# Four-quarter inverse products in the RWKV-7 stage, spaced reloads on the SP queue, and halved weight splits in the sliding-window stage

## The reference, cut to what matters

```
def step(state, inp):
    r_t, w_t, k_t, v_t, kk_t, a_t = inp
    sa = jnp.einsum("bhvk,bhk->bhv", state, -kk_t)
    state = (state * w_t[:, :, None, :]
             + sa[..., None] * (kk_t * a_t)[:, :, None, :]
             + v_t[..., None] * k_t[:, :, None, :])
    y = jnp.einsum("bhvk,bhk->bhv", state, r_t)
    return state, y
```

## Time and profile before

| | us |
|---|---|
| median of 3 runs | 1948.91 |
| lowest and highest | 1947.67, 1950.61 |
| the profiled execution: its own time | 1947.52 |
| its span | 1945.6 |
| around the span | 1.9 |
| PE busy | 1919.5 (99%) |
| DVE busy | 1332.9 (69%) |
| ACT busy | 838.4 (43%) |
| RWKV-7 products, first to last | 204.91 to 383.42 |

### The profile page before, as it was taken

The page is one execution under the profiler, slowest core; times in us unless marked ns, Lnnn a source line. Parts: engine busy times, 40 slices in busy tenths (PEclk is TensorE's granted clock), DMA queues, the critical chain, the costliest instruction groups (busy, mean ns, idle before and its releaser), DMA issues.

```text
span 1945.6 us, 32866 instructions
## 1 busy us (share of the span) xinstructions
PE 1919.5 (99%) x14082; PEld 1653.4 (85%) x14082; DVE 1332.9 (69%) x1751; ACT 838.4 (43%) x1257; POOL 118.7 (6%) x126
## 2 busy tenths in 40 slices
PE   8999999999999999999999999999999999999998
PEld 6877897888788998978989888898887778898897
DVE  5576868576687777676545687677566768777665
ACT  4243744254453444443324454344345545344342
POOL 1155100000000000020000000000002300000000
PEclk9999999999999999999999999999999999999999
DMA  8222404137132332333220223233242113233231
GB/s 270 88 65 66 136 10 143 36 120 130 44 109 87 109 104 92 104 94 108 89 86 26 84 89 107 87 108 109 87 139 73 49 44 109 87 108 109 87 108 44
DMA packets 138641, 182.12 MB, mean 94 GB/s; under 512 B 4853, under 2 KB 103365, under 8 KB 138112
## 3 DMA queue, kind: packets, MB, share of 16 engines
q1 hardware_dynamic: 135392, 168.91, 26.8%
q0 software_dynamic: 3104, 11.11, 2.8%
HBM read 172.66 MB, written 7.34 MB: 93 GB/s over the span
## 4 chain that ended last, share of the span: by engine, by line
PE 94%; DVE 3%; ACT 1%; issue 1%; DMA 0%; DVEq 0%; ACTq 0%
PE X L1579 20%; PE M L1491 19%; PE M L1492 19%; PE M L1493 19%; PE X L642 3%; PE M L1552 1%; PE M L1554 1%; PE M L1553 1%; PE M L1905 1%; PE X L1882 1%; PE X L1762 1%; PE X L1893 1%; PE X L1731 1%; DVE w_lo L2372 1%; PE X L1493 0%
## 5 line engine op out<-in xcount | busy, mean ns | idle before, releaser
L1492 PE MATMUL M<-u,raw_lo 128*128 128x512 f32 x728 | 287.9, 396 | 0.0
L1491 PE MATMUL M<-u,w_hi 128*128 128x512 f32 x728 | 287.9, 395 | 0.0
L1493 PE MATMUL M<-u,w_hi 128*128 128x512 f32 x728 | 286.1, 393 | 0.0
L1995 ACT ACTIVATE w_hi<-raw 128x2048 fp32r<-128x2048 f32 x113 | 215.6, 1908 | 96.2 <-PE M L1554 43.5
L2050 ACT ACTIVATE us<-X 128x256 f32<-128x256 f32 x156 | 60.2, 386 | 426.9 <-PE X L1579 426.9
L2522 DVE TENSOR_TENSOR h<-h,M 128x512 f32<-128x512 f32 x184 | 123.7, 685 | 144.6 <-PE M L1493 144.5
L1579 PE MATMUL X<-t,w_hi 128*128 128x256 f32 x936 | 173.2, 282 | 0.0
L1493 PEld LDWEIGHTS M<-u,w_hi 128*128 128x128 f32 x728 | 137.6, 189 | 32.8
L1491 PEld LDWEIGHTS M<-u,w_hi 128*128 128x128 f32 x728 | 136.8, 188 | 30.8
L1492 PEld LDWEIGHTS M<-u,raw_lo 128*128 128x128 f32 x728 | 136.7, 188 | 29.8
L2372 DVE TENSOR_TENSOR w_lo<-raw,w_hi 128x2048 fp32r<-128x2048 f32 x56 | 128.1, 2289 | 32.5 <-ACT w_hi L1995 32.5
(11 more groups left out here) (529 smaller groups left out, 4564.5 us busy)
## 6 DMA issues: line engine op xcount, KB each, us to landing
raw<-in_w_up_dram SPq DMA_DIRECT2D x48, 1024.0 KB, 5.4
raw<-in_w_down_dram SPq DMA_DIRECT2D x48, 1024.0 KB, 5.1
raw<-in_w_in_dram SPq DMA_DIRECT2D x12, 1024.0 KB, 8.3
raw<-in_a_w_in_dram SPq DMA_DIRECT2D x12, 1024.0 KB, 5.3
h<-in_x_dram SPq DMA_DIRECT2D x16, 256.0 KB, 7.7
raw<-in_w_mk_dram SPq DMA_DIRECT2D x4, 1024.0 KB, 5.1
raw<-in_w_mv_dram SPq DMA_DIRECT2D x4, 1024.0 KB, 5.4
raw<-in_w_out_dram SPq DMA_DIRECT2D x4, 1024.0 KB, 6.5
```

Of the source, the lines that this page charges most:

```text
L1491: mm(dst, wh, xh, start=start, stop=False)
L1492: mm(dst, wl, xh, start=False, stop=False)
L1493: return mm(dst, wh, xl, start=False, stop=stop)
L1995: nc.scalar.activation(hi_of(n)[:, :, :], raw[:, n % 4], ACT.Copy).then_inc(S["w_hi_ready"], 1)
```

## The change

Three edits go together.

**Products on four quarters.** `P2`, `PT2`, `P4`, `PT4` and `TT2` join `RW_QUAD`. The first two read blocks on the chunk's rows and write to the head's rows (`to_heads`); the others read on the head's rows and write back to the chunk's (`to_chunks`). Since `TT2` now needs its right operand on head rows, a new product `PTH` (`P` times the identity, four quarters) makes it for each pair, and DVE adds the identity when it takes it out of PSUM. The three order tables are new. PSUM readers take two banks as one operand (`rw_wide`), same elements as before.

```diff
-RW_QUAD = ("L", "RBT", "AKT", "RKT", "MT", "RT", "N", "Y")
+RW_QUAD = ("L", "RBT", "AKT", "RKT", "MT", "RT", "N", "Y", "P2", "PT2", "PTH", "P4", "PT4", "TT2")
-    tA.0.0 fill.22 bonus.1.2 fill.23 tBd.1.1 RBT.0.2 PT2.0.3 P2.0.1 RBT.1.2 P2.1.3 PT2.1.0 PT4.0.1 TT2.0.2 P4.0.0 PT4.1.3
+    fill.14 fill.15 kk2.1.1 fill.16 fill.17 fill.18 bonus.0.0 tKd.0.1 L.0.1 AKT.0.2 tA.0.0 kk2.2.1 tBd.0.0 fill.19 X.0.2 P2.0.2
...
+            to_heads = dict(P2=("PT", "P"), PT2=("P", "PT"), PTH=("P", "I"))
+            to_chunks = dict(P4=("PT2", "P2"), PT4=("P2", "PT2"), TT2=("P2", "PTH"))
...
+                elif st in to_heads or st in to_chunks:
+                    for cp in range(4):
+                        for turn in range(2):
+                            for cpar in range(2):
+                                hh, at_ = cpar ^ turn, (hp, cpar ^ turn, cp, cpar)
+                                if st in to_chunks:
+                                    a_, b_ = (by_row(n, *at_) for n in to_chunks[st])
+                                    last = mm(quad(st, hp, hh, cpar, cp), a_, b_, start=True, stop=True)
+                                else:
+                                    a_, b_ = (by_chunk(n, *at_) for n in to_heads[st])
+                                    last = mm(quad(st, hp, cpar, hh, cp), a_, b_, start=True, stop=True)
...
+                elif op == "PTH":
+                    mm_done("X", hp)
+                    go(TTO(by_head(s_("PTH")), rw_pair(op, hp), mask2("eye64"), ALU.add))
                 elif op in ("TT2", "TT3", "TT4", "TT5", "TT6"):
-                    go(TTO(s_("TT"), b_[:], s_("TT"), ALU.add))
+                    go(TTO(two(s_("TT")), b_, two(s_("TT")), ALU.add))
```

```diff
-            for c in range(KT):
-                if c == 4:
-                    load_wide(N_WOB, mix_w, 0)
+
+            def reload(c):
                 sp.dma_start(h[:, c, :], A["x"][:, c, :]).then_inc(S[f"ld_x{c}"], 16)
+
+            for c in range(4):
+                reload(c)
+            sp.wait_ge(S["acc_evac"], ACC[N_WOA] + 1)
+            load_wide_part(N_WOB, mix_w, 0, 0)
+            sp.wait_ge(S["acc_evac"], ACC[N_WOA] + 2)
+            for c in range(4, KT):
+                reload(c)
+            sp.wait_ge(S["acc_evac"], ACC[N_WOA] + 4)
+            load_wide_part(N_WOB, mix_w, 0, 1)
+            sp.wait_ge(S["acc_evac"], ACC[N_WOA] + 5)
             load_plain(N_MQ)
```

```diff
+                    if qb == 2 and c - 3 in HI_SW:
+                        lo_half(HI_SW[c - 3], 1)
                     if qb % 2 == 0:
                         dve.wait_ge(S["sw_score"], u + 2)
...
-                if c in HI_SW:
+                if c in HI_SW and c + 3 < KT:
+                    lo_half(HI_SW[c], 0)
+                elif c in HI_SW:
                     lo(HI_SW[c])
```

More of the change, by code:

```diff
@@ new lines @@
+RW_PE = """zw.0.0 za.0.1 zw.1.2 za.1.3 fill.9 zw.2.4 za.2.5 zw.3.0 za.3.1 fill.10 dn.0.2 fill.11 tV.1.0 tV.0.1 kk2.0.3 fill.12 fill.13
+    fill.14 fill.15 kk2.1.1 fill.16 fill.17 fill.18 bonus.0.0 tKd.0.1 L.0.1 AKT.0.2 tA.0.0 kk2.2.1 tBd.0.0 fill.19 X.0.2 P2.0.2
+    PTH.0.0 RBT.0.1 PT2.0.2 fill.20 tKd.1.0 TT2.0.1 P4.0.2 PT4.0.0 RKT.0.1 TT3.0.4 P8.0.0 L.1.1 AKT.1.2 TT4.0.0 fill.21
+    bonus.1.1 tA.1.2 fill.22 tBd.1.0 PT2.1.1 Z.0.1 P2.1.2 RKT.1.1 TT5.0.0 RBT.1.2 PT4.1.1 X.1.1 Z2.0.0 PTH.1.2 P4.1.1 TT6.0.0
+    TT2.1.2 P8.1.1 W.0.0 TT3.1.2 G.0.1 MT.0.2 TT4.1.0 N.0.1 RT.0.2 Z.1.0 S1.0.1 fill.23 S2.0.0 TT5.1.1 S3.0.0 fill.24 S4.0.0
+    Z2.1.1 S5.0.0 kk2.3.2 S6.0.0 TT6.1.1 Y.0.2 G.1.0 W.1.1 var.0.3 tV.2.1 fill.25 gate.0.0 fill.26 MT.1.1 N.1.2 fill.27
+    bonus.2.1 S1.1.2 tKd.2.3 fill.28 fill.29 S2.1.0 AKT.2.1 RT.1.2 S3.1.0 fill.30 S4.1.0 fill.31 S5.1.0 RKT.2.1 L.2.2 S6.1.0
+    X.2.1 Y.1.1 tV.3.0 var.1.4 tBd.2.5 fill.32 tA.2.4 fill.33 fill.34 gate.1.2 fill.35 PT2.2.2 RBT.2.1 PTH.2.0 P2.2.2 fill.36
+    PT4.2.1 P4.2.2 TT2.2.0 L.3.1 fill.37 tKd.3.0 tA.3.1 fill.38 tBd.3.0 TT3.2.1 AKT.3.1 P8.2.0 PT2.3.2 P2.3.1 TT4.2.0 X.3.1
+    PTH.3.1 Z.2.0 RBT.3.2 P4.3.1 TT5.2.0 PT4.3.1 TT2.3.2 Z2.2.0 P8.3.1 TT3.3.2 TT6.2.0 RKT.3.2 TT4.3.1 fill.39 Z.3.1 W.2.0 G.2.2
+    TT5.3.1 MT.2.2 RT.2.1 Z2.3.0 N.2.2 TT6.3.0 bonus.3.1 S1.2.0 G.3.4 S2.2.0 W.3.5 S3.2.0 N.3.1 MT.3.2 S4.2.0 fill.40 S1.3.0
+    RT.3.1 S5.2.4 S2.3.0 fill.41 S6.2.0 S3.3.2 fill.42 S4.3.0 Y.2.1 S5.3.0 gate.2.4 var.2.0 S6.3.5 fill.43 Y.3.0 fill.44
+    gate.3.2 fill.45 var.3.3 fill.46 fill.47""".split()
@@ new lines @@
+RW_DVE = """w.2 cs.1 cs.0 t.0 t.1 ev.4 dl.0 csx.0 kmod.1 csx.1 kk2.0 dn.0 ev.5 dl.1 kmod.0 ev.6 w.3 kk.0 rk.0 kk2.1 K.0 Kd.0 ev.7 beta.0 B.0
+    A.0 ev.8 Bd.0 kk.1 bonus.0 Kd.1 L.0 AKT.0 R.0 kk2.2 PT.0 w.4 PTH.0 RBT.0 beta.1 K.1 rk.1 TT2.0 A.1 Bd.1 B.1 RKT.0 TT3.0 R.1
+    AKT.1 ev.9 L.1 PT.1 TT4.0 bonus.1 T4.0 ev.10 w.5 RKT.1 TT5.0 RBT.1 T5.0 PTH.1 TT6.0 TT2.1 TT3.1 yd.0 MT.0 TT4.1 RT.0 S1.0
+    T4.1 S2.0 S3.0 TT5.1 S4.0 S5.0 T5.1 S6.0 ev.11 kk.2 TT6.1 t.2 beta.2 w.6 cs.2 kk2.3 csx.2 kmod.2 var.0 dl.2 rk.2 K.2 MT.1
+    ev.12 yb.0 Kd.2 A.2 R.2 yc.0 Bd.2 bonus.2 S1.1 ev.13 yd.1 gate.0 yd.2 S2.1 yd.3 S3.1 RT.1 B.2 AKT.2 S4.1 S5.1 ev.14 RKT.2
+    S6.1 L.2 w.7 t.3 ev.15 kmod.3 cs.3 kk.3 dl.3 var.1 beta.3 rk.3 csx.3 yb.1 PT.2 ev.16 yc.1 gate.1 A.3 RBT.2 K.3 yr.0 PTH.2
+    B.3 TT2.2 Kd.3 Bd.3 ev.17 R.3 yr.1 L.3 PT.3 TT3.2 AKT.3 TT4.2 PTH.3 T4.2 RBT.3 TT5.2 T5.2 TT2.3 ev.18 TT3.3 RKT.3 TT4.3
+    TT6.2 ev.19 T4.3 w.8 TT5.3 MT.2 T5.3 TT6.3 S1.2 RT.2 S2.2 S3.2 S4.2 MT.3 S1.3 RT.3 S2.3 S5.2 S6.2 ev.20 S3.3 S4.3 S5.3 w.9
+    S6.3 bonus.3 var.2 yb.2 yc.2 gate.2 yr.2 ev.21 ev.22 var.3 yb.3 ev.23 yc.3 gate.3 w.10 yr.3""".split()
@@ L806, in rwkv_act @@
                         dve("RBT", hp)
-                    go(sl("Z" if op == "Z2" else op, hp)[:], rw_bank(op, hp)[:], ACT.Copy)
+                    go(two(sl("Z" if op == "Z2" else op, hp)[:]), rw_wide(op, hp), ACT.Copy)
         def rwkv_dve(dve, lo, fill_out):
@@ L838, in mask2 @@
                 return C(name).unsqueeze(1).unsqueeze(1).to_broadcast([P, 2, 4, 64])
-            products = {"L", "RBT", "AKT", "RKT", "kk2", "bonus", "TT2", "TT3", "TT4", "TT5", "TT6", "MT", "RT"} | {f"S{i}" for i in range(1, 7)}
+            products = {"L", "RBT", "AKT", "RKT", "kk2", "bonus", "PTH", "TT2", "TT3", "TT4", "TT5", "TT6", "MT", "RT"} | {f"S{i}" for i in range(1, 7)}
             for op, hp in RW_OPS["d"]:
```

114 lines of the change are left out of this document (55 added, 59 removed).

## The result

The changed kernel takes 1955.50 us (median of 22 runs, 1950.69 to 1961.83); the kernel before, measured on the same chips, 1950.05 (22 runs, 1947.67 to 1958.20). The ratio is 1.0023 with a 95% interval of 1.0013 to 1.0033, so 2.5 to 6.4 us slower, 4.5 at the middle. I had forecast 5.7 us faster. The profiled execution of the changed kernel took 1956.07, near its median; its span is 1954.3, that of before 1945.6, so the two traces differ by 8.7, more than the ratio.

What follows compares the result with a forecast made beforehand. The prediction took PE, busy 1919.5 of 1945.6 us, as the bound; −7.3 + 4.8 − 2.1 + 0.6 − 1.7 = −5.7 us gave 1941.8 from the profiled execution (1943.2 from the median), range 1939.5 to 1945.0.

Steps and rivals of the forecast that it cites:

- Products: PE in the changed stage: 20 products on four quarters save 9.2 us, four added PTH cost 1.9; together −7.3 us.
- part 2: The forecast's term for PE's instruction fetching in dense stretches: +4.8 us, bounds 0 and +7.3.
- Fetching: Four dense PE stretches wait for instruction blocks, 3.5 us per 256 instructions: 6.6 us, less 1.8 in the old order, +4.8.
- Rival A: Instruction fetching on PE doesn't limit, blocks come sooner when asked faster: −11.5 us in all, 1937.4; chance 0.16.
- rival B: Fetching eats the four-quarter products' gain whole: −3.2 us left, or −1, 1945.7 to 1947.9; chance 0.26.
- Spaced reload: SP's 5 MB reload split into groups of at most 1 MB removes PE's idle: −3.1, +1.0 allowed back, −2.1 us.
- The +1.0: Allowance in the reload term, in us, because the spaced groups now fall among four-quarter products.
- Waits of the new order: PE waits for banks and evacuations in the reordered stage: +0.6 us, bounds 0 and +4.
- Rival C: Pair 0, run ahead alone, is bound by latency, up to 0.5 us at some 12 steps: about 1952; chance 0.06.
- Halved splits: Sliding-window stage: halving DVE's 2.28 us split removes PE's waits for logits, 0.89 + 0.79: −1.7 us, bounds −1.7 and 0.

Runs made afterwards that it cites:

- e12: Changed kernel with its five products back on two quarters and PTH removed, keeping new order, spaced reload and halved splits: 1949.74 us, ratio 1.0013.
- e10: Kernel before with the halved splits and x reloaded chunk by chunk: 1945.85 us, ratio 0.9986.
- e11: Changed kernel without an edit, run again on another chip: 1952.94 us, ratio 1.0024 to the kernel before.
- e8: Kernel before with the spaced reload and the halved splits, without four-quarter products and new order: 1946.13 us, ratio 0.9981.
- e9: As e12, with the four PTH products back on PE and in DVE, their result unused: 1955.39 us, ratio 1.0042.
- e1: Changed kernel with the reload of x, WOB and MQ issued in one row again: 1951.13 us, ratio 1.0018 to the kernel before.
- e5: Kernel before with bare 64x64 matmuls added after its last store, queues empty or loaded: 3.74 us per 256 instructions when fetch-bound.
- e2: Kernel before with the spaced reload alone: 1947.08 us, ratio 1.0000.
- e3: Kernel before with the halved splits of the sliding-window stage alone: 1946.36 us, ratio 0.9993.

## Why the prediction was wrong

The terms of the sum can be set beside the runs of one chip, by medians. The second row is e12 less e10, the third e11 less e12 (e10 has the finer reload; e8, with the spaced one, gained as much):

| | forecast | measured |
|---|---|---|
| halved splits and spacing, in the old order (e10) | −1.7 − 2.1 = −3.8 | −3.0 |
| the new order, on two quarters | +0.6 | +3.9 |
| four quarters and PTH, with their fetching | −7.3 + 4.8 = −2.5 | +3.2 |
| sum | −5.7 | +4.1 |

So the steps that failed are the price of fetching for the four-quarter products and PTH, in which the stalls behind the spaced reload are contained, and the cost of the order.

**Products (−7.3).** The saving was right for the 20 products: 8.1 to 9.8 us of busy time between e9 and e11, forecast 9.2. PTH was mis-sized: I took 4 x 0.47 = +1.9, which is its work (2.0), where e9 against e12 shows 4.7 to 5.65 by medians, loosely. In a dense stretch its 64 instructions are what counts (0.94 us each, 3.7 in all), and it lies in the densest part. That makes my upper bound for part 2 wrong too: if no four-quarter product is faster than a two-quarter one, the 20 gain nothing and the four PTH cost 3.7, so the bound is 7.3 + 3.7 = +11.0 and not +7.3.

**Fetching (+4.8).** The mechanism was right and so were the stretches: idles inside products, 3.7 us apart, from tBd.1 to S1.0, 3.5 us in sum where I had 2.8. For the whole stage I had 6.6 of such idles before taking off the 1.8 of the old order; e1, with the reload in one row, has 6.7 in its trace, and the changed kernel 12.3 by its single idles, of which 6.2 are the three idles behind the groups of SP. So the pace was about right, and what was missing stands in the next part. Where PE runs dry the interval is 3.74 on average and not 3.5. Rival A fell (e5), rival B, which I gave 0.26, was nearest: the price of fetching about eats the gain. It was still short of the result, for it had PTH inside the products' gain and nothing for the order.

**Spaced reload (−2.1).** I argued from the earlier trace rows that 5 MB in a row delay PE's block, which e5 confirms (idles 5.3 us longer with four quarters, 3.0 with two), and that smaller groups would cost less. In the old order that roughly held (2.62 us of idle became 1.23 in e2, though the time shows no sure gain). In the new order it failed: the traces have it the other way round, and by times the forecast gain of 2.1 is not there (e1 is 1 us better by ratios, which isn't resolved). I did not ask what PE does where each group lands. In the new order the single row (SP issues it from 304.7 to 312.2 in e1) falls where fills 32 to 35 stand and costs 0.64; the spaced groups fall beside four-quarter products and cost 1.56 and 2.27. The +1.0 that I had allowed for this was too little. It may also make the time uneven: whether a block is asked for just before or just after four chunks of x decides, as I read the two traces, between an idle of 0.37 (e11's trace) and 2.40 (this one), both at the same matmul.

**Waits of the new order (+0.6).** I counted waits, and they were of the size that I said, +1.2 (2.6 us after, 1.4 before), though most of it is a bank that I hadn't named: gate.0's, before S2.1. I did not count changes of tile size. With products on two quarters the new order costs 4 us by medians against e10 (1949.74 and 1945.85): 2.3 of busy time, which 14 changes would account for, and 1.7 of idle, two thirds of it waits. Rival C, latency of pair 0's chain, is not it: the longest waits for readers of that chain are 0.57 and 0.31.

**Halved splits (−1.7).** About right: −1.4 in e3 by medians, its interval just reaching no change, and the idle gone from the trace.

**The clock** was in none of my cases. In the shown trace it adds some 2.7 us of busy time behind the two longest idles; in e11's trace of the same kernel nothing. With the longer idles that is why this stage is 4.2 us longer than e11's, and why the one execution stood 8.7 above before where the ratio says 4.5.

The parts by the ratios, times 1948.8: halves and spacing −2.7 (e10) to −3.7 (e8); the new order +5 (e12 over e10); PTH +5.7 (e9 over e12); four quarters −3.5 (e11 over e9). The four of one chip add up to the 1.0024 of e11, +4.7, by construction. The intervals of the single ratios are 3 to 5 us wide, and e9's is 8, so the first two parts are good to 2 or 3 us, and PTH and the four quarters only as a sum (+2.1 by ratios, +3.2 by medians).

## What to carry to other kernels

A stream of small matmuls has a floor per instruction: here 256 instructions in 3.74 us, 29 ns for a matmul and its weight load. Count instructions per microsecond before spreading matmuls over more of the array, and price an added product by its instructions. Four quarters pay 0.46 us a product only where long matmuls stand between (a fill for two products; 0.42 with one for four, in a short row), and by the traces transfers should be put where PE has few instructions to fetch, not simply apart. Count the changes of tile size in a new order (0.17 us each in the probe), and the banks that it makes neighbours share. The version to keep is the kernel before with the halved splits and either form of spacing (ratio 0.9981 and 0.9986); it was the change's modest parts that held.
